# Where the delta stage takes the norms of keys and queries: from products with ones to decay exponents, value rows and the result's norm

## The chip, the cores and the metric

The kernel runs on one core of a Trainium2 chip. Its engines are TensorE (PE, matmuls, with its weight loads PEld), VectorE (DVE), ScalarE (ACT), GpSimd (POOL) and SyncE (SP, which issues DMAs). Each runs its own instructions in program order and waits on semaphores for the others. The metric is the device time of one execution in microseconds (us); several executions of a kernel are timed and the median counts.

## The reference

One layer of an encoder on 1024 tokens of width 2048. One projection feeds three groups of heads: A, a gated DeltaNet with eight heads of 128 in both directions; B, windowed attention; C, cross-attention into 256 memory tokens. The change is all in group A:

```python
def l2_norm(t):
    return t * lax.rsqrt(jnp.sum(t * t, axis=-1, keepdims=True) + EPS)
...
qa = l2_norm(qa); ka = l2_norm(ka)
...
q = q * dk ** -0.5
decay = jnp.where(incl, jnp.exp(gc_i - gc_j), 0.0)
a = -jnp.where(strict, (k * beta) @ k.T * decay, 0.0)
tinv = (I - a) ** -1
u = tinv @ (v * beta);  w = tinv @ (k * beta * jnp.exp(gc))
qk = q @ k.T * decay;   q_dec = q * jnp.exp(gc)
k_dec = k * jnp.exp(gc_last - gc)
v_new = u - w @ state;  o = q_dec @ state + qk @ v_new
state = state * jnp.exp(gc_last) + k_dec.T @ v_new
...
o_a = rms_norm(o_fwd + o_bwd, o_norm_a) * silu(za)
```

A key's norm is a factor per token. It can be left on the raw key if the decay of its column is divided by the squared norm and its value row is multiplied by the norm. A query's norm is a factor on one row of `o`, which the RMS norm of the result takes out again, up to its epsilon.

## The kernel before

`front_stage` makes the projections and stores them as tiles of 128 by 1024. `delta_stage` (from L569) takes the eight heads of group A one after another; then come the attention stage (B and C) and the output projection. Each engine's program in the delta stage is written out by hand: `heads(slot)` calls `slot(h, parity, more, before)` for the eight heads. `more` is true for h = 0 to 6 and marks that the head after this one (g = h + 1) is prepared inside the slot; `before` is true for h = 1 to 7 and marks that the head before this one is finished inside it (its RMS norm and gate). No scheduler is at work: what stands in a slot runs in that order on its engine.

A slot has two parts. The first inverts the triangular matrices of head h in six levels (L = 6). In each level TensorE multiplies four banks (`products_z`, L1240), VectorE masks them (`take_z`, L1055), TensorE multiplies again (`products_i`, L1246), and VectorE adds the result in (`take_i`, L1069) and transposes it for the next level (`turn`, L1063). The second part is a scan over eight chunks. Between these products TensorE does the work for head g, all of it in one pair of PSUM banks `pp`, and VectorE, ScalarE and GpSimd do theirs:

- ScalarE squares queries and keys (`squares`, L746); TensorE adds the squares up by a product with a tile of ones (`norm_sums`, L1178); ScalarE makes the root from Ln and Exp (`roots`, L752 and L755), and VectorE multiplies the tiles by it (`unit`, L1034). Ln and Exp come from two table sets, so an ACT_TABLE_LOAD stands before each change.
- VectorE's `columns` (L1021 to L1029) are five instructions on 8 to 32 elements per partition: they make the decay exponents of the columns. The last, `kdc`, is the exponent of the keys that go into the state.
- GpSimd's `neg_rows` (L940, two instructions) makes the decay exponents of the rows in `dec`, which ScalarE exponentiates (`decays`, L769). After it come `end` (L984, L987: the finished head times its norm, times its gate), `decayed_queries` (L950), `scaled_rows` (L959) and `first_inverse` (L968 to L974).
- The head before is finished by ScalarE squaring its result (`end_squares`, L802), TensorE's `end_sums` (L1220), ScalarE's `end_roots` (L807, L810) and `end_take` (L817), and GpSimd's `end`.

The first head has no slot before it; its preparation stands in front of `heads(slot)` on each engine. In the last slot (h = 7) ScalarE and TensorE prepare the attention stage instead of a next head (`early_squares`, `early_sums`, L837 and L1308).

## Time and profile before

| | us |
|---|---|
| median of 3 runs | 2295.89 (2295.61 to 2296.03) |
| span of the profiled execution | 2292.6 |
| delta stage, its first load issued to its last VectorE instruction | 1202.7 to 1758.9 |
| one slot, h = 1 to 6 | 60.27 |
| ScalarE busy, of the span | 667.5 |
| VectorE busy, of the span | 1058.1 |

Of the profiled execution the page gives only the span, 3.3 us less than the median; what lies around the span is not itemised. A TensorE product of 128x128 in fp32 counts as two records and takes one slot of 0.22 us at the full clock, so "x16" in a row of the trace are eight products. Times in a timeline are counted from the start of the span.

### The profile page before, as it was taken

Reading aid. Unit: us, or ns where it says so; the run is one execution under the profiler, and the core shown is the slowest. Engines: PE = TensorE matmul, PEld = TensorE weight load, DVE = VectorE, ACT = ScalarE, POOL = GpSimd, SP = SyncE. Lnnn points to the kernel's source line nnn. Section 1 sums busy time; section 2 is a strip of 40 time slices with the busy share of each in tenths; the row PEclk is TensorE's granted clock in tenths of the full one; section 3 lists DMA queues with packets and bytes.
Section 4 is the critical chain, followed back from the end, with each engine's and each line's share of the span. In section 5 each row is a group of like instructions: output and inputs, shape, how many; then the busy total and the mean of one; then the engine's idle time right before and its main releaser. Section 6 shows DMA issues by size and latency. Waiting matters only on the chain. (4 is left out here: it accounts for less than half of the span.)

```text
span 2292.6 us, 28450 instructions
## 1 busy us (share of the span) xinstructions
PE 2160.5 (94%) x11264; PEld 1800.8 (79%) x11264; DVE 1058.1 (46%) x1834; ACT 667.5 (29%) x1019; POOL 337.8 (15%) x208
## 2 busy tenths in 40 slices
PE   6999999999999999999985999999998778999998
PEld 6788888888888888888873888888886445888887
DVE  7764344354353311122315666666644887422222
ACT  6511111111111111111105455555543665311111
POOL 4300000000000000000003455555511000000000
PEclk9999999999999999999996999999979999999999
DMA  6522221221221221221203131111111333634432
GB/s 224 192 92 68 70 82 58 79 82 55 82 77 61 82 82 64 73 82 56 65 28 122 47 123 66 65 65 65 47 65 55 101 90 122 230 132 165 143 128 91
DMA packets 78866, 210.87 MB, mean 92 GB/s; under 512 B 7328, under 2 KB 33056, under 8 KB 74560
## 3 DMA queue, kind: packets, MB, share of 16 engines
q1 hardware_dynamic: 69232, 174.57, 22.9%
q0 software_dynamic: 9552, 35.19, 3.9%
q8 instruction: 53, 0.87, 0.2%
q14 instruction: 29, 0.24, 0.0%
HBM read 165.11 MB, written 44.63 MB: 91 GB/s over the span
## 5 line engine op out<-in xcount | busy, mean ns | idle before, releaser
L73 PE MATMUL pr_acc<-x_hi,pr_w_lo 128*128 128x512 f32 (+1 forms) x1760 | 675.5, 384 | 27.0 <-DVE pr_w_lo L432 24.4
L75 PE MATMUL pr_acc<-x_hi,pr_w_hi 128*128 128x512 f32 (+1 forms) x1760 | 673.9, 383 | 0.0
L74 PE MATMUL pr_acc<-x_lo,pr_w_hi 128*128 128x512 f32 (+1 forms) x1760 | 673.8, 383 | 0.0
L73 PEld LDWEIGHTS pr_acc<-x_hi,pr_w_lo 128*128 128x128 f32 x1760 | 333.6, 190 | 92.8 <-issue 18.6
L74 PEld LDWEIGHTS pr_acc<-x_lo,pr_w_hi 128*128 128x128 f32 x1760 | 333.8, 190 | 63.7 <-issue 0.2
L75 PEld LDWEIGHTS pr_acc<-x_hi,pr_w_hi 128*128 128x128 f32 x1760 | 333.7, 190 | 63.6
L348 ACT ACTIVATE pr_w_hi<-pr_w_raw 128x1024 fp32r<-128x1024 f32 x118 | 124.8, 1059 | 749.3 <-PE pr_acc L75 730.4
L533 DVE TENSOR_TENSOR pr_padded<-pr_acc,pr_rstd 128x512 f32<-128x512 f32 x82 | 56.6, 692 | 518.4 <-PE pr_acc L75 518.3
L256 POOL DMA_DIRECT2D proj_scratch<-pr_res x49 | 26.2, 535 | 1010.0 <-DVE pr_res L556 829.3
L432 DVE TENSOR_TENSOR pr_w_lo<-pr_w_raw,pr_w_hi 128x1024 fp32r<-128x1024 f32 x118 | 147.8, 1289 | 0.2 <-ACT pr_w_hi L348 0.2
L545 DVE SCALAR_TENSOR_TENSOR pr_conv<-pr_padded,pr_head_taps,pr_conv 128x1024 f32<-128x1024 f32 x96 | 123.3, 1285 | 3.4
L1240 PE MATMUL dl_ring<-dl_wt,dl_mt 128*128 128x128 f32 x768 | 107.2, 290 | 9.1 <-DVE dl_wt L1063 9.1
L1240 PEld LDWEIGHTS dl_ring<-dl_wt,dl_mt 128*128 128x128 f32 x768 | 97.0, 199 | 20.8 <-DVE dl_wt L1063 12.7
L1069 DVE TENSOR_TENSOR dl_dt<-dl_ring,dl_dt 128x256 f32<-128x256 f32 x192 | 78.9, 412 | 48.2 <-PE dl_ring L1246 45.8
L1246 PEld LDWEIGHTS dl_ring<-dl_dt,dl_wt 128*128 128x128 f32 x768 | 95.2, 198 | 7.5 <-issue 7.5
L73 PE MATMUL ou_acc<-ou_w_hi,ou_lo_rest 128*128 128x512 f32 x256 | 99.6, 389 | 0.0
L74 PE MATMUL ou_acc<-ou_w_lo,ou_hi_rest 128*128 128x512 f32 x256 | 99.6, 389 | 0.0
L75 PE MATMUL ou_acc<-ou_w_hi,ou_hi_rest 128*128 128x512 f32 x256 | 99.6, 389 | 0.0
L1246 PE MATMUL dl_ring<-dl_dt,dl_wt 128*128 128x128 f32 x768 | 98.4, 283 | 0.0
L1055 DVE TENSOR_TENSOR dl_wt<-dl_ring,c_masks 128x256 f32<-128x256 f32 x192 | 76.0, 417 | 33.7 <-PE dl_ring L1240 32.0
L533 DVE TENSOR_TENSOR pr_res<-pr_acc,pr_rstd 128x512 f32<-128x512 f32 x20 | 13.8, 692 | 167.4 <-PE pr_acc L75 167.3
L1911 DVE TENSOR_TENSOR c_ow_lo<-c_e_pair,c_ow_hi 128x2048 fp32r<-128x2048 f32 x15 | 34.4, 2294 | 121.2 <-ACT c_ow_hi L1875 121.2
(263 smaller groups left out, 2939.4 us busy)
## 6 DMA issues: line engine op xcount, KB each, us to landing
pr_w_raw<-in_w_in SPq DMA_DIRECT2D x118, 512.0 KB, 5.2
proj_scratch<-pr_res POOLq DMA_DIRECT2D x49, 512.0 KB, 5.4
c_e_more<-in_w_out SPq DMA_DIRECT2D x16, 1024.0 KB, 5.0
c_e_pair<-in_w_out SPq DMA_DIRECT2D x15, 1024.0 KB, 4.9
dl_qk<-proj_scratch SPq DMA_DIRECT2D x8, 1024.0 KB, 5.0
dl_grow<-gate_rows SPq DMA_DIRECT2D x8, 1024.0 KB, 7.6
c_e_q_in<-in_x SPq DMA_DIRECT2D x8, 1024.0 KB, 7.2
out<-c_e_kvt POOLq DMA_DIRECT2D x8, 1024.0 KB, 4.7
```

The source lines that it names most:

```text
L73: pe.matmul(out, w_lo, x_hi, start=first, stop=False)
L74: pe.matmul(out, w_hi, x_lo, start=False, stop=False)
L75: return pe.matmul(out, w_hi, x_hi, start=False, stop=last)
L348: return act.activation(w_hi[:, b], w_raw[:, b], ACT.Copy).then_inc(s_hi, 1)
L432: dve.tensor_tensor(w_lo[:, b], w_raw[:, b], w_hi[:, b].bitcast(F32), ALU.subtract).then_inc(s_lo, 1)
L533: dve.tensor_tensor(body[:, bass.ts(h, HALF)], acc[:, bank + h], rstd[:, bass.ts(h, HALF)], ALU.mult).then_inc(s_taken, 1)
L545: dve.scalar_tensor_tensor(conv[:], src, w, conv[:], ALU.mult, ALU.add).then_inc(s_tap, 1)
L1055: dve.tensor_tensor(zz[:, 2 * b:2 * b + 2], ring[:, b, 0:2 * P].rearrange("p (a n) -> p a n", n=P), masks[:, level, None, :].to_broadcast( ...
L1069: dve.tensor_tensor(left, as_blocks(ring[:, b, 0:2 * P], LEVELS[level]), left, ALU.add).then_inc(s_id, 1)
L1240: last = pe.matmul(ring[:, b, bass.ts(i, P)], mt[:, 2 * b + i], d[:, 2 * b + i], start=True, stop=True)
L1246: last = pe.matmul(as_blocks(ring[:, b, bass.ts(i, P)], LEVELS[level]), zz[:, 2 * b + i], left_d(parity, 2 * b + i, 1, level), start=True, ...
L1911: dve.tensor_tensor(w_lo[q % 2], w_raw[q % 2], w_hi[q % 2].bitcast(F32), ALU.subtract).then_inc(w_l, 1)
```

## The change

Keys and queries stay raw. Their squares are no longer summed by a product with ones.

- Keys: TensorE transposes the raw keys already at level 0 (`to_rows(g, 0)`). ScalarE reads each half twice from PSUM: once squared into the tile `kd`, which is free then, and once copied into `k_rows`. VectorE sums the squares (`key_sums`, one TENSOR_REDUCE, level 1), ScalarE takes the logarithm of the 8 sums per partition (`key_logs`), VectorE subtracts it from the column exponents and makes `kdc` (`key_columns`, two small instructions, level 2), and ScalarE makes the norm (`value_scales`), by which it multiplies the value rows, chunk by chunk (`value_rows`, now eight instructions).
- Queries: ScalarE squares them (`query_squares`), and when the head is finished GpSimd adds these squares to those of the result (`add_queries`) ahead of `end_sums`. For the last head VectorE adds them.
- One table set with both Ln and Exp is loaded before the first head; from there to the last slot no other is. ACT_TABLE_LOADs in the delta stage: 49 before, 7 now.
- `norm_sums`, `roots`, `unit` and their semaphores are gone.

The core of the diff:

```diff
             def slot(h, parity, more, before):          # ScalarE
                 g, q = h + 1, 1 - parity
-                if more:
-                    squares(g)
                 if before:
                     end_squares(h - 1)
-                if not more:
+                if more:
+                    key_rows(g, q, pp)
+                    query_squares(g, q)
+                else:
                     early_squares()
                 if more:
-                    roots(g, 1)
-                if more:
-                    roots(g, 0)
+                    key_logs(g)
                 if before:
                     end_roots(h - 1)
                     end_take(h - 1)
                 if more:
-                    key_rows(g)
+                    value_scales(g)
                     column_exps(g, q)
                     row_exps(g)
                 if more:
-                    value_rows(g, q)
+                    value_rows(g, q, pp)
                     decays(g, 0, 5)
...
+            def key_rows(g, parity, bank):
...
+                    turned = bank[:, half].rearrange("p (a n) -> p a n", n=P)
+                    act.activation(key_squares(parity)[:, 4 * half:4 * half + 4], turned, ACT.Square).then_inc(e_ksq, 1)
+                    act.activation(k_rows[:, 4 * half:4 * half + 4], turned, ACT.Copy).then_inc(e_rows, 1)
...
+            act.preload_act_table_set("natural_log_exp_and_others")
...
+            def add_queries(f, parity):                 # GpSimd
+                pool.wait_ge(f_sq, f * 2 + 2)
+                pool.wait_ge(e_sq, f + 1)
+                pool.tensor_tensor(osq[:], osq[:], root[:, parity], ALU.add).then_inc(f_ad, 1)
...
             def slot(h, parity, more, before):
+                if before:
+                    add_queries(h - 1, 1 - parity)
                 if more:
                     neg_rows(h + 1)
...
+            def key_sums(g, parity):                    # VectorE
+                dve.wait_ge(e_ksq, g * 2 + 2)
+                dve.tensor_reduce(ksum[:], key_squares(parity), AX_X, ALU.add).then_inc(e_ks, 1)
+
+            def key_columns(g):
+                dve.wait_ge(e_kln, g + 1)
+                dve.wait_ge(e_dif, g * 3 + 1)
+                dve.tensor_tensor(negc[:], negc[:], kln[:, None, :].to_broadcast([P, 2, NC]),
+                                  ALU.subtract).then_inc(e_dif, 1)
+                dve.wait_ge(e_dif, g * 3 + 2)
                 dve.tensor_tensor(kdc[:], glast[:], negc[:], ALU.add).then_inc(e_dif, 1)
...
                     if more and level == 1:
-                        unit(g, 1)
+                        key_sums(g, q)
+                    if more and level == 2:
+                        key_columns(g)
...
-                    if more and level == 1:
-                        unit(g, 0)
...
                     if more and level == 0:             # TensorE
-                        norm_sums(g, 1)
+                        to_rows(g, 0, None)
                     if more and level == 2:
-                        to_rows(g, 0, h - 1 if before else None)
+                        to_rows(g, 1, h - 1 if before else None)
...
                         if more:
-                            end_sums(h - 1, e_rt, g * 4 + 4)
+                            end_sums(h - 1, e_rows, g * 4 + 2)
...
-                    if more and level == 0:
-                        norm_sums(g, 0)
-                    if more and level == 2:
-                        to_rows(g, 1, None)
```

How the instructions stand, on VectorE in the slot of head 1 before the change, from the masking of level 0 to the adding of level 2 (`dl_wt<-dl_ring` is `take_z`, `dl_dt<-dl_ring` is `take_i`):

```order
L1055 TENSOR_TENSOR dl_wt<-dl_ring,c_masks 128x256 x4
L1021 COPY dl_hc<-c_cols 128x32
L1023 COPY dl_glast<-dl_grow 128x8
L1024 COPY dl_glast<-dl_grow 128x8
L1027 TENSOR_TENSOR dl_negc<-dl_hc 128x16
L1029 TENSOR_TENSOR dl_kdc<-dl_glast,dl_negc 128x16
L1069 TENSOR_TENSOR dl_dt<-dl_ring,dl_dt 128x64x2x2 x2
...
L1055 TENSOR_TENSOR dl_wt<-dl_ring,c_masks 128x256 x4
L1034 SCALAR_TENSOR_TENSOR dl_qk<-dl_qk,dl_root 128x1024
...
L1034 SCALAR_TENSOR_TENSOR dl_qk<-dl_qk,dl_root 128x1024
L1055 TENSOR_TENSOR dl_wt<-dl_ring,c_masks 128x256 x4
L1069 TENSOR_TENSOR dl_dt<-dl_ring,dl_dt 128x16x2x8 x2
```

The same stretch of VectorE with the change (L1078 is `take_z`, L1092 is `take_i`):

```order
L1078 TENSOR_TENSOR dl_wt<-dl_ring,c_masks 128x256 x4
L1040 COPY dl_hc<-c_cols 128x32
L1042 COPY dl_glast<-dl_grow 128x8
L1043 COPY dl_glast<-dl_grow 128x8
L1046 TENSOR_TENSOR dl_negc<-dl_hc 128x16
L1092 TENSOR_TENSOR dl_dt<-dl_ring,dl_dt 128x64x2x2 x2
...
L1078 TENSOR_TENSOR dl_wt<-dl_ring,c_masks 128x256 x4
L1050 TENSOR_REDUCE dl_ksum<-dl_kd 128x8
L1092 TENSOR_TENSOR dl_dt<-dl_ring,dl_dt 128x32x2x4 x2
...
L1078 TENSOR_TENSOR dl_wt<-dl_ring,c_masks 128x256 x4
L1055 TENSOR_TENSOR dl_negc<-dl_negc,dl_kln 128x16
L1058 TENSOR_TENSOR dl_kdc<-dl_glast,dl_negc 128x16
L1092 TENSOR_TENSOR dl_dt<-dl_ring,dl_dt 128x16x2x8 x2
```

Two passes over 1024 elements have gone and one has come; one small instruction of level 0 has moved to level 2, with a new one ahead of it.

On GpSimd, before the change, from the end of the slot of head 0 to the decayed queries in the slot of head 1 (`dl_dec` is `neg_rows`, `c_e_pair` is `end`, which works in that tile):

```order
L974 TENSOR_TENSOR dl_mt<-dl_mt 128x1024
L940 TENSOR_TENSOR dl_dec<-dl_grow,c_neg 128x1024 x2
L984 TENSOR_TENSOR c_e_pair<-c_e_pair,dl_osq 128x1024
L987 TENSOR_TENSOR c_e_pair<-c_e_pair,dl_z 128x1024
L950 TENSOR_TENSOR dl_qd<-dl_qk,dl_grow 128x1024 x2
```

And with the change:

```order
L986 TENSOR_TENSOR dl_mt<-dl_mt 128x1024
L997 TENSOR_TENSOR dl_osq<-dl_osq,dl_root 128x1024
L952 TENSOR_TENSOR dl_dec<-dl_grow,c_neg 128x1024 x2
L1002 TENSOR_TENSOR c_e_pair<-c_e_pair,dl_osq 128x1024
L1005 TENSOR_TENSOR c_e_pair<-c_e_pair,dl_z 128x1024
L962 TENSOR_TENSOR dl_qd<-dl_qk,dl_grow 128x1024 x2
```

The new addition stands ahead of the two instructions of `neg_rows`, in the slots of heads 1 to 6.

## Rows read from the trace of the kernel before

**Rows 1.** The page, its first line.

```profile
span 2292.6 us, 28450 instructions
```

**Rows 2.** Busy time in a stretch: length, then us per engine (instructions), clock, DMA.

```profile
1190.00:1700.00 510.00, 460.82 (x3421) 412.05 (x3420) 325.93 (x818) 251.55 (x424) 252.25 (x115) 0.96 0.22 75
```

**Rows 3.** Timeline of TensorE, head 1: start, duration, line [idle before <- releaser].

```profile
1306.55 1.95 PE L1240 MATMUL dl_ring<-dl_wt,dl_mt 128*128 128x128 f32 x16
1308.34 1.88 PE L1178 MATMUL dl_pp<-dl_root,c_ones 128*128 128x512 f32 x4
...
1315.94 1.99 PE L1220 MATMUL dl_pp<-dl_osq,c_ones 128*128 128x512 f32 x4 [0.30 <-ACT dl_root L752]
```

**Rows 4.** Timeline of VectorE, the same slot, levels 0 to 2.

```profile
1307.20 1.76 DVE L1055 TENSOR_TENSOR dl_wt<-dl_ring,c_masks 128x256 f32<-128x256 f32 x4
...
1310.73 0.91 DVE L1069 TENSOR_TENSOR dl_dt<-dl_ring,dl_dt 128x256 f32<-128x256 f32 x2 [1.11 <-PE dl_ring L1246]
...
1318.41 0.87 DVE L1069 TENSOR_TENSOR dl_dt<-dl_ring,dl_dt 128x256 f32<-128x256 f32 x2 [1.18 <-PE dl_ring L1246]
...
1321.19 1.18 DVE L1034 SCALAR_TENSOR_TENSOR dl_qk<-dl_qk,dl_root 128x1024 f32<-128x1024 f32 x1
...
1324.01 0.87 DVE L1069 TENSOR_TENSOR dl_dt<-dl_ring,dl_dt 128x256 f32<-128x256 f32 x2 [0.30 <-PE dl_ring L1246]
```

**Rows 5.** Timeline of GpSimd, the same slot.

```profile
1301.87 4.66 POOL L940 TENSOR_TENSOR dl_dec<-dl_grow,c_neg 128x1024 f32<-128x1024 f32 x2
1324.50 2.40 POOL L984 TENSOR_TENSOR c_e_pair<-c_e_pair,dl_osq 128x1024 f32<-128x1024 f32 x1 [17.97 <-ACT c_e_pair L817]
```

**Rows 6.** Timeline of ScalarE, the same slot.

```profile
1306.75 1.08 ACT L802 ACTIVATE dl_osq<-dl_po 128x512 f32<-128x512 f32 x2 [13.62 <-PE dl_po L1296]
...
1319.57 1.27 ACT L807 ACTIVATE dl_osq<-dl_pp,c_scalars 128x512 f32<-128x512 f32 x2
1320.85 1.28 ACT L810 ACT_TABLE_LOAD   x1
```

**Rows 7.** Timeline of GpSimd and VectorE in the slot of head 0.

```profile
1248.27 4.68 POOL L940 TENSOR_TENSOR dl_dec<-dl_grow,c_neg 128x1024 f32<-128x1024 f32 x2 [0.84 <-DMA dl_grow<-gate_rows]
1248.32 2.34 DVE L1023 COPY dl_glast<-dl_grow 128x8 f32<-128x8 f32 x1
...
1250.57 0.16 DVE L1024 COPY dl_glast<-dl_grow 128x8 f32<-128x8 f32 x1
1250.77 2.22 DVE L1027 TENSOR_TENSOR dl_negc<-dl_hc 128x16 f32<-128x16 f32 x1
```

**Rows 8.** Timeline of GpSimd and VectorE at the kernel's start.

```profile
14.67 4.36 POOL L236 TENSOR_TENSOR pr_rstd<-pr_rstd,pr_padded 128x1024 f32<-128x1024 f32 x2 [1.23 <-ACT pr_padded L360]
...
14.83 2.08 DVE L442 TENSOR_SCALAR x_hi<-pr_conv,pr_mem_nw 128x256 fp32r<-128x256 f32 x1
...
17.10 2.08 DVE L442 TENSOR_SCALAR x_hi<-pr_conv,pr_mem_nw 128x256 fp32r<-128x256 f32 x1
```

**Rows 9.** Busy time and granted clock in short stretches before and in head 0.

```profile
1216.00:1218.00 2.00, 0.19 (x1) 0.00 (x0) 0.70 (x2) 1.81 (x3) 0.50 (x1) 1.00 0.00 0
1218.00:1220.00 2.00, 0.00 (x0) 0.00 (x0) 0.68 (x1) 1.99 (x3) 0.00 (x0) 0.60 0.00 0
...
1248.00:1250.00 2.00, 2.00 (x8) 1.23 (x7) 1.77 (x2) 1.40 (x3) 1.73 (x1) 0.72 0.95 389
```

**Rows 10.** Timeline of ScalarE, VectorE and TensorE before the first slot.

```profile
1216.56 0.17 DVE L1029 TENSOR_TENSOR dl_kdc<-dl_glast,dl_negc 128x16 f32<-128x16 f32 x1
...
1220.45 4.77 ACT L769 ACTIVATE dl_dec<-dl_dec,dl_negc 128x128 f32<-128x128 f32 x16
...
1229.37 2.35 DVE L1145 TENSOR_TENSOR dl_dt<-dl_mt,c_level 128x1024 f32<-128x1024 f32 x2
...
1236.13 3.78 PE L1240 MATMUL dl_ring<-dl_wt,dl_mt 128*128 128x128 f32 x16 [7.23 <-DVE dl_wt L1063]
```

**Rows 11.** Groups of instructions: a reduction over 1024 elements, attention stage.

```profile
L1624 DVE TENSOR_REDUCE at_mx<-at_ps 128x4 f32<-128x1024 f32 x8 | 9.8, 1219 | 0.0
```

More of the change, by code:

```diff
@@ L14 @@
 from contextlib import ExitStack
+import math
 import numpy as np
@@ L906, in slot @@
                     early_rotation()
[L908 to L916 removed]
+            act.preload_act_table_set("natural_log_exp_and_others")
+            key_rows(0, 0, po)
+            key_logs(0)
+            value_scales(0)
             column_exps(0, 0)
@@ L919, in _ @@
             row_exps(0)
-            for which, dst in enumerate((k_rows, v_rows[:, 0])):
-                for half in range(2):
-                    act.wait_ge(e_tr, 2 * which + half + 1)
-                    act.activation(dst[:, 4 * half:4 * half + 4], po[:, half].rearrange("p (a n) -> p a n", n=P),
-                                   ACT.Copy, scale=0.5 if which else 1.0).then_inc(e_rows, 1)
+            value_rows(0, 0, ring)
+            query_squares(0, 0)
             heads(slot)
@@ L1128, in _ @@
             columns(0)
-            unit(0, 1)
-            unit(0, 0)
+            key_sums(0, 0)
+            key_columns(0)
             dve.wait_ge(l_on, 16)
@@ L1158, in _ @@
             dve.wait_ge(f_st, f * 16)
-            dve.wait_ge(f_sq, f * 2 + 2)
+            dve.wait_ge(e_sq, A_HEADS)
+            for half in range(2):
+                cols_ = bass.ts(half, HALF)
+                dve.wait_ge(f_sq, f * 2 + (half + 1))
+                dve.tensor_tensor(osq[:, cols_], osq[:, cols_], root[:, parity, cols_], ALU.add).then_inc(f_ad, 1)
             for half in range(2):
@@ L1372, in slot @@
                         early_rotate(1)
-            for j in (1, 0):
-                pe.wait_ge(e_sq, 1 - j + 1)
-                for half in range(2):
-                    pe.matmul((pp if j else ring)[:, half], c["ones"][:], root[:, j, bass.ts(half, HALF)],
-                              start=True, stop=True).then_inc(e_nm, 1)
-            pe.wait_ge(e_hat, E0 + 1)
+            pe.wait_ge(l_qk, 16)
+            for half in range(2):
+                for i in range(4):
+                    last = pe.transpose(po[:, half, bass.ts(i, P)], qk[:, 1, bass.ts(4 * half + i, P)], ident[:])
+                last.then_inc(e_tr, 1)
             for half in range(2):
@@ L1394, in _ @@
             pe.wait_ge(l_v, 16)
-            for which, rows in enumerate((qk[:, 1], v[:])):
-                for half in range(2):
-                    if which:
-                        pe.wait_ge(e_rows, half + 1)
-                    for i in range(4):
-                        last = pe.transpose(po[:, half, bass.ts(i, P)], rows[:, bass.ts(4 * half + i, P)], ident[:])
-                    last.then_inc(e_tr, 1)
+            for half in range(2):
+                for i in range(4):
+                    last = pe.transpose(ring[:, half, bass.ts(i, P)], v[:, bass.ts(4 * half + i, P)], ident[:])
+                last.then_inc(e_tr, 1)
+            pe.wait_ge(e_rows, 4)
             heads(slot)
```

110 lines of the change are left out of this document (48 added, 62 removed).

## Prediction, made before the changed kernel ran

> **What bounds the kernel now.** I started at the page's span [rows 1], then asked for busy time by stretch, and in the delta stage for the timelines of the engines in the slot of head 1, which heads 2 to 6 repeat every 60.27 us. TensorE is busy 460.8 of the 510 us that hold the stage's first part, VectorE 325.9, ScalarE 251.6, GpSimd 252.3 [rows 2]. That looks like a stage bound by TensorE, and over a whole slot it nearly is. But I read level by level, with S = 1306.55 as the slot's start [rows 3]. A level needs 3.6 us of TensorE (8 products in 1.79, twice) and about 4.4 us of VectorE (mask 4, add 4, transpose 4). Only where TensorE has extra work, or VectorE has, does a level take longer. So the levels are a ring through both engines, and a stall of VectorE between its masking and its adding lengthens the slot as soon as TensorE has no other work to cover it.
>
> **What goes.** `norm_sums` is two pairs of products of 1.71 us each at level 0 [rows 3]; the transposes of the keys (eight records where a group of products has sixteen, so 0.9 us) move up into one of the places. `unit` is two passes of VectorE, 1.18 to 1.22 us each, and a reduction of 1.2 us takes the place of one [rows 4, 11]. 42 ACT_TABLE_LOADs go, but ScalarE is hardly waited for inside a slot; what this is worth is seen below. If nothing else happened I get this for a slot: adding at level 0 starts at S + 3.4 instead of S + 4.2 [rows 4], level 1 at S + 9.2 instead of S + 11.9, level 2 at S + 14.5 instead of S + 17.5. A gain of 2.9 us per slot; this is a rival below.
>
> **What comes, and where it falls.** The place that decides is VectorE's `columns` at level 0, which starts when the masking ends, S + 2.35 (1307.20 + 1.76 is S + 2.41, less the overlap of neighbours) [rows 4]. Before the change GpSimd is idle then: `neg_rows` ran from 1301.87 to 1306.53, before the slot, and `end` came at 1324.50 [rows 5]. With the change `add_queries` stands ahead of `neg_rows` and waits for the squares of the result, done at S + 1.28 (1306.75 + 1.08) [rows 6]. So GpSimd works S + 1.3 to 3.7, 3.7 to 6.05 and 6.05 to 8.4 (2.34 us an instruction) [rows 7], right over `columns`.
>
> What such an overlap does is in the trace, in the slot of head 0, where `columns` falls on `neg_rows`: a copy of 8 elements takes 2.34 us and a subtraction of 16 takes 2.22 us, each until the GpSimd instruction of that moment ends; the copy behind the first one slips through in 0.16 us [rows 7]. At the kernel's start it is the same with four equal instructions under two of GpSimd: the first waits 2.08 us, the second passes, the third waits 2.08 us, the fourth passes [rows 8]. VectorE's instructions that read PSUM and one SBUF tile (masking, adding, `attention`), and its transposes, ran beside GpSimd at their usual length.
>
> The Trainium skill, page "SBUF — State Buffer", section "Who interferes with whom", says that VectorE and GpSimd share a pair of ports, that a two-port copy or an instruction with two SBUF inputs and a GpSimd instruction lock each other out for a whole instruction, and that whoever issues first wins. It speaks against this change, which puts one more GpSimd instruction first; rows 7 agree with it at 2.34 and 2.22 us. By the rule the sum is the forecast's, without it the first rival's.
>
> So with the change, at level 0: the first copy waits until S + 3.7, the second passes, the third waits until S + 6.05, and the subtraction, which waits for the copies' semaphore and starts 0.2 us behind the last one [rows 7], comes too late for the gap and waits until S + 8.4. Adding starts at S + 8.45 instead of S + 4.2.
>
> Level 1: adding and transposing take 2.66 us, masking 1.35, the reduction 1.2, so the key sums are there at T = S + 13.65. TensorE's next products start 1.15 us after adding began and are done at S + 11.6; `end_sums` (1.7 us) follows, then `products_i`, so that adding starts at S + 14.0 instead of S + 11.86 [rows 4].
>
> Level 2: `key_columns` comes 4.1 us after that (2.78 for adding and transposing, 1.33 for masking), at S + 18.1. On ScalarE `end_roots` now stands behind `key_logs`; from its first Ln to GpSimd's start it took 4.93 us with one table load of 1.28 [rows 5, 6], so 3.65 without, so GpSimd's `end` starts at T + 3.8 = S + 17.45, ahead of VectorE by 0.6 us. Both of its instructions (2.4 us each) [rows 5] stop one of the two of `key_columns`, since the second again waits for a semaphore: free at S + 22.4. Adding starts there instead of at S + 17.46 [rows 4]. Levels 3 to 5 and the scan follow as before. The loss is 4.9 us per slot, six times.
>
> Bounds of this term: if the first copy is not stopped, the subtraction gets through at S + 6.05 and the same reckoning gives +2.6 per slot; if nothing is stopped, -2.9. I take 4.9, because a copy of the same kind was stopped.
>
> **TensorE's clock.** The stalls leave TensorE without work from S + 4.6 to S + 9.6, and for some 3.6 us before level 3. In the trace an idle time that began at 1216.2 finds the mean clock at 0.60 in the stretch from 1218 on [rows 9]: it fell from 2.4 to 1.2 GHz in it. The eight products that came first after an idle time of 7.23 us took 3.78 us [rows 10] instead of 1.95 [rows 3], so at least that much work goes at 1.2 GHz; in the slot of head 0 the clock is on its way back only in the stretch from 1248 on, at 0.72 [rows 9]. For the first idle time that is 0.7 to 2.2 us, for the second 0 to 1.4, since VectorE sets the pace there. Bounds 0 to 3.6 per slot; I take 1.3, the low half, because the low clock covers a piece of one group only.
>
> **The other terms.** In front of head 0, VectorE's `columns` still ends at 1216.56 [rows 10]; then come the reduction 1.2, two small ScalarE and two small VectorE steps, together 1.2, so the 16 decays (4.77 us) start at 1218.95 instead of 1220.45 and end at 1223.7 [rows 10]. Products of keys with keys no longer wait for norms, so only the decays are waited for, and VectorE's last matrix is ready at 1224.65 instead of 1229.37 [rows 10]: -4.7 us, and the loads for head 1 come as much earlier. The table load on this path is 1.3 us of it. The value rows, now last on ScalarE, are ready at 1228.2, before the slot starts at 1231.4, and cost nothing; bounds -5 to -2. In the slot of head 0, `columns` is stopped by `neg_rows` as before [rows 7]; one `unit` goes (-1.2), two small steps come, TensorE has less to do and comes to level 1 with the clock low (+1.0): -0.2, bounds -1.5 to +2. In head 7's slot TensorE's clock falls and returns as before as far as the rows tell. Behind the last scan VectorE adds in halves ahead of each product, 0.6 us [rows 11].
>
> Sum: 6 x (4.9 + 1.3) - 4.7 - 0.2 + 0.6 = +32.9. On the span of 2292.6 [rows 1] that is 2325.5, and 3.3 us more on the median of 2295.89, which stands that far above it: 2328.8 us, 1.4% slower.
>
> **Rivals.**
> 1. No new stall: VectorE gets in between GpSimd's instructions, or these come later than I think. For it: inside the slots of heads 1 to 6 no stop was ever seen; against it, both engines' starts follow from rows, and the same two pieces of work did stop each other in head 0. Then 6 x -2.9 - 4.7 - 1.1 + 0.6 = -22.6: 2273 us. That is the change doing what it says.
> 2. Half the stops: level 0 is left at S + 6.05, no clock loss. 6 x 2.6 - 4.3 = +11: 2307 us. If `key_columns` is moreover ahead of `end` (it is 0.4 us behind in this case), one of its two stops goes, 2.4 us per slot: -3, 2293 us. This needs only half a microsecond.
> 3. The clock takes its whole price, low after both idle times in each slot: 6 x 8.5 - 4.3 = +47: 2343 us. If it stayed low through the levels, more than 2350.
> 4. ScalarE becomes late: its value rows are eight instructions of some 0.3 us instead of two, and its row exponents come behind `key_columns`. In my reckoning the value rows end at S + 27.2 and TensorE asks for them at S + 30.4; a margin of 3 us. If it fails, +1 us per slot, 2335 us, inside the range.
>
> **The numbers.** Forecast with the stops in full, clock price from 0 to 3 us: 0.56 (2318 to 2339). Rival 2, its first case: 0.17; its second, at no change or just under: 0.05. Rival 3: 0.10, of it 0.03 over 2350. Rival 4: 0.03. Rival 1: 0.09. The range from 2303 to 2348 leaves out rival 1, rival 2's second case and the top of rival 3. This kernel's measurement can tell 0.2% (4.6 us) from no change. Faster: rival 1 and a part of rival 2's second case, 0.11; within 0.2%: 0.03; slower: 0.86.
>
> **What the profile after would show.** Right: in the slots of heads 1 to 6 a VectorE copy on `glast` or `hc` of 1.4 to 2.4 us, a subtraction on `negc` of over 2 us at level 0 and one or two at level 2; slots of 65 to 68 us instead of 60.27; idle TensorE of about 5 us behind level 0 and a clock under 1.00 somewhere behind it; ScalarE with fewer busy us and nobody waiting for it. Wrong: these instructions at 0.17 us, or slots under 60 us. If they are long and the slots are still short, then my order of levels is wrong; if slots are over 69 us, the clock costs more than I took.

## The result and the profile after

The changed kernel took 2312.86 us (median of 6 runs, 2301.4 to 2314.72), the kernel before, run beside it, 2295.96 us: a ratio of 1.0067, with a 95% interval of 1.0048 to 1.0085. The change makes the kernel slower by 17 us. I had forecast +32.9 us. The direction was right, and the time lies in the range, but the loss is half of what I summed up.

The profiled execution of the changed kernel took 2312.98 us. First line of its page:

```profile
span 2311.3 us, 28308 instructions
```

That is 18.7 us over [rows 1]. The same stretch of the delta stage as in [rows 2]: length, then busy us of TensorE, its weight loads, VectorE, ScalarE and GpSimd with their instructions, granted clock, DMA share, GB/s.

```profile
1190.00:1700.00 510.00, 434.58 (x3262) 401.14 (x3261) 345.08 (x798) 164.95 (x398) 263.82 (x120) 0.92 0.20 69
```

TensorE has 26 us less work in it and ScalarE 87 us less, and still the stage is longer: VectorE is busy 19 us more with fewer instructions. Fewer instructions that take longer: that is where to look. The slots begin (first products of level 0) at 1231.44, 1302.24, 1365.95, 1430.00, 1494.45, 1557.96, 1621.69 and 1685.87, so the six middle ones take 383.6 us, 63.9 each (63.5 to 64.5), where they took 361.6, 60.27 each. The 18.7 us are:

| part | forecast | measured |
|---|---|---|
| in front of head 0 | -4.7 | -4.7 |
| slot of head 0 | -0.2 | +0.4 |
| slots of heads 1 to 6 | +37.2 | +22.0 |
| last slot and end of the stage | +0.6 | +0.3 |
| all later stages | 0 | +0.7 |

The timeline of VectorE in the slot of head 1 (start, duration, engine, line; S = 1302.24), which answers to [rows 4, 7]:

```profile
1304.57 1.44 DVE L1040 COPY dl_hc<-c_cols 128x32 f32<-128x32 f32 x1
1305.92 0.16 DVE L1042 COPY dl_glast<-dl_grow 128x8 f32<-128x8 f32 x1
1306.00 2.33 DVE L1043 COPY dl_glast<-dl_grow 128x8 f32<-128x8 f32 x1
1308.36 2.27 DVE L1046 TENSOR_TENSOR dl_negc<-dl_hc 128x16 f32<-128x16 f32 x1
1310.55 0.74 DVE L1092 TENSOR_TENSOR dl_dt<-dl_ring,dl_dt 128x256 f32<-128x256 f32 x2
...
1322.12 1.21 DVE L1055 TENSOR_TENSOR dl_negc<-dl_negc,dl_kln 128x16 f32<-128x16 f32 x1
1323.36 0.17 DVE L1058 TENSOR_TENSOR dl_kdc<-dl_glast,dl_negc 128x16 f32<-128x16 f32 x1
```

GpSimd in the same slot (the answer to [rows 5]; in brackets the idle time before an instruction and what ended it):

```profile
1303.60 2.37 POOL L997 TENSOR_TENSOR dl_osq<-dl_osq,dl_root 128x1024 f32<-128x1024 f32 x1 [6.02 <-ACT dl_osq L821]
1305.92 4.67 POOL L952 TENSOR_TENSOR dl_dec<-dl_grow,c_neg 128x1024 f32<-128x1024 f32 x2
1320.94 2.36 POOL L1002 TENSOR_TENSOR c_e_pair<-c_e_pair,dl_osq 128x1024 f32<-128x1024 f32 x1 [10.35 <-ACT c_e_pair L836]
1323.38 2.40 POOL L1005 TENSOR_TENSOR c_e_pair<-c_e_pair,dl_z 128x1024 f32<-128x1024 f32 x1
```

Read the two together by their ends. The first copy ends where `add_queries` does, the third instruction with the first of `neg_rows`, the subtraction with the second. The first of `key_columns` ends where GpSimd's first multiplication by the norm does, but the second takes only 0.17 us: it starts at 1323.36, and GpSimd's next instruction, which waits for the semaphore of the one ahead of it, at 1323.38.

TensorE, the answer to [rows 3]:

```profile
1302.24 1.95 PE L1258 MATMUL dl_ring<-dl_wt,dl_mt 128*128 128x128 f32 x16
...
1311.70 3.78 PE L1258 MATMUL dl_ring<-dl_wt,dl_mt 128*128 128x128 f32 x16 [4.71 <-DVE dl_wt L1086]
```

And its granted clock, the third number from the end of a line, in stretches of 2 us:

```profile
1310.00:1312.00 2.00, 0.30 (x1) 0.30 (x2) 2.00 (x6) 0.00 (x0) 0.59 (x1) 0.50 0.00 0
1312.00:1314.00 2.00, 2.00 (x11) 2.00 (x11) 1.78 (x6) 0.00 (x0) 0.00 (x0) 0.50 0.00 0
1314.00:1316.00 2.00, 2.00 (x8) 1.61 (x8) 1.14 (x4) 0.00 (x0) 0.00 (x0) 0.51 0.00 0
1316.00:1318.00 2.00, 2.00 (x10) 1.22 (x9) 1.07 (x2) 0.90 (x3) 0.00 (x0) 1.00 0.00 0
```

It waits 4.71 us for VectorE and comes back at 1.2 GHz (granted clock 0.50) for some 4 us; the same eight products take 3.78 us instead of 1.95. There is no second fall in the slot. The wait is 4.71 or 4.72 us in all six middle slots, but the time for which the clock stays at 0.50 after it is 3.2 to 6.2 us, and the slots follow it: the one of head 4 with 3.2 us takes 63.5 us, the one of head 3 with 6.2 us takes 64.5.

### The profile page after: what moved, and what is told of

Same layout as the page of the kernel before. It is cut to its first block and busy times, and to the rows that moved or that the text cites. A ratio compares the mean times of both kernels' runs of the same rounds, so it can differ in the third digit from the quotient of the medians.

```text
span 2311.3 us, 28308 instructions
## 1 busy us (share of the span) xinstructions
PE 2151.8 (93%) x11200; PEld 1804.9 (78%) x11200; DVE 1086.7 (47%) x1838; ACT 589.0 (25%) x1001; POOL 354.9 (15%) x215
## 5 line engine op out<-in xcount | busy, mean ns | idle before, releaser
L1258 PE MATMUL dl_ring<-dl_wt,dl_mt 128*128 128x128 f32 x768 | 122.6, 314 | 48.0 <-DVE dl_wt L1086 47.8
L1258 PEld LDWEIGHTS dl_ring<-dl_wt,dl_mt 128*128 128x128 f32 x768 | 108.4, 219 | 60.3 <-DVE dl_wt L1086 38.7
L1092 DVE TENSOR_TENSOR dl_dt<-dl_ring,dl_dt 128x256 f32<-128x256 f32 x192 | 77.8, 410 | 38.6 <-PE dl_ring L1264 36.7
L1078 DVE TENSOR_TENSOR dl_wt<-dl_ring,c_masks 128x256 f32<-128x256 f32 x192 | 74.9, 414 | 35.9 <-PE dl_ring L1258 34.8
```

The source lines that it names most:

```text
L1078: dve.tensor_tensor(zz[:, 2 * b:2 * b + 2], ring[:, b, 0:2 * P].rearrange("p (a n) -> p a n", n=P), masks[:, level, None, :].to_broadcast( ...
L1092: dve.tensor_tensor(left, as_blocks(ring[:, b, 0:2 * P], LEVELS[level]), left, ALU.add).then_inc(s_id, 1)
L1258: last = pe.matmul(ring[:, b, bass.ts(i, P)], mt[:, 2 * b + i], d[:, 2 * b + i], start=True, stop=True)
```

## The experiments

Each was run beside the kernel before, whose own runs lie in two groups, near 2282 and near 2295 us (experiment 8 goes into this). The changed kernel has such groups too: four of its six runs lie near 2313.6 us and two near 2301.6. So I read each kernel's middle slots in its trace first, and its median second. Where the clock doesn't fall in them the middle slots repeat within 0.1 us, except where I say so.

**1. Masked rows first.** Does the order on GpSimd make the loss?

```diff
-                if before:
-                    add_queries(h - 1, 1 - parity)
                 if more:
                     neg_rows(h + 1)
+                if before:
+                    add_queries(h - 1, 1 - parity)
```

> The changed kernel with two operations of GpSimd exchanged in each slot: the masked rows of the next head (neg_rows) come before the adding of the query squares (add_queries), not behind it. Theory (the 16.9 us are port stops, and what TensorE's clock loses in the idle time that they open): the masked rows run before the slot's start, as in the kernel before, and only the adding is left beside the copies of `columns`. The first copy is stopped until about S + 3.7, the other three instructions run in 0.1 to 0.2 us each, the first `take_i` adds at about S + 4.2 instead of S + 8.3, TensorE's idle of 4.72 us in level 0 goes and with it the fall of the clock to 0.50. Middle slots: 63.9 less 4.1 less 1.7 = about 58.1 us; the run about 2313 - 6 x 5.8 = 2278 us (2273 to 2288). Rival A (the loss comes from the added work itself, on VectorE's key sums and ScalarE's eight value rows, and the stops only take time that was idle anyway): the slots stay near 63.9 us, the run 2308 to 2315 us. Rival B (the stops go, but the clock falls all the same, since the slot's load on TensorE is now lighter): slots about 59.8 us, the run about 2288 us.

Measured: slots of 58.14 us, 2278.11 us (2266.95 to 2285.48, 7 runs), ratio to before 0.9929 (0.9902 to 0.9956). Of the four instructions only the first is stopped, 1.44 us; adding starts at S + 4.05 and TensorE never waits over 0.7 us in a middle slot. The theory holds to a tenth of a microsecond per slot; rivals A and B fall.

**2. A pause between the two masked-row instructions.** Why did the second of `key_columns` get through?

```diff
                 for direction in range(2):
+                    if after_first(g) and direction == 1:
+                        pool.wait_ge(e_neg, g * 2 + 1)
                     pool.tensor_tensor(dec[:, direction * NC:(direction + 1) * NC],
```

> The changed kernel with one wait added: between the two masked-row instructions of GpSimd, the second waits for the semaphore of the first (for the middle heads and head 7's slot alike). Nothing else moves. Theory (an instruction of VectorE gets through where GpSimd pauses on a semaphore, which is why only one of the two of key_columns was stopped): the pause of some 0.05 us lets the subtraction behind the copies, stopped for 2.27 us in every middle slot of the changed kernel, run in 0.1 to 0.2 us. The first `take_i` adds at about S + 6.1 instead of S + 8.3, TensorE's idle falls from 4.7 to about 2.5 us, and the slot gains 2.2 us, with the clock's 1.7 us if it no longer falls: 6 x 2.2 to 6 x 3.9 = 13 to 23 us, the run 2290 to 2300 us. Rival (the pause plays no part, the second of key_columns got through for another reason, such as its smaller size or because two stops don't follow each other): the subtraction is still stopped for about 2.3 us, the run stays at 2311 to 2314 us.

Measured: slots of 61.25 to 61.43 us, 2299.25 us (2296.01 to 2303.37). VectorE in the slot of head 1:

```profile
1306.70 2.33 DVE L1045 COPY dl_glast<-dl_grow 128x8 f32<-128x8 f32 x1
1309.06 0.18 DVE L1048 TENSOR_TENSOR dl_negc<-dl_hc 128x16 f32<-128x16 f32 x1
```

GpSimd's pair takes 4.83 us instead of 4.67, 0.16 us more, and the subtraction 0.18 instead of 2.27. One added wait on GpSimd makes the slot 2.5 us shorter, of which 2.1 us are the earlier adding (S + 6.2 instead of S + 8.3). TensorE's idle time is 2.62 us, and its clock still falls (0.50 for one stretch of 2 us in the slot of head 2), so most of the clock's price stays. The rival falls. In the slot of head 0 the same wait stands between the same two instructions, and there it doesn't help: VectorE's subtraction comes 0.06 us after GpSimd's second instruction has started, and takes 2.31 us.

**3. Keep TensorE busy in the idle time.** What does the clock cost apart from the stops?

```diff
                     for b in range(4):
                         products_i(h, parity, level, b)
+                    if more and before and level == 0:
+                        pe.wait_ge(e_rows, g * 4 + 2)
+                        for i in range(5):
+                            pe.matmul(pp[:, i % 2], c["ones"][:], qk[:, 1, 0:HALF], start=True, stop=True)
```

> The changed kernel with five products more on TensorE in each middle slot, whose results nobody reads: ones x keys, 512 columns each, behind the products of level 0 that wait for take_z, so that they fall into the idle time of 4.72 us. The stops of the port are untouched. Theory (the idle time costs twice, once as a delay and once as a clock that falls to 0.50 behind it, 1.7 us per slot as read): the granted clock stays at 1.00 between S + 8 and S + 18, the second adding comes at about S + 14.0 instead of S + 15.7, slots about 62.2 us, the run about 2313 - 10 = 2303 us (2299 to 2306). Rival (the clock's fall costs nothing, since VectorE's instructions set level 1 and not TensorE's products): the clock stays up and the run stays at 2311 to 2315 us. Second rival (the five products delay the next level's, which stand behind them in TensorE's queue): slower than 2315 us.

Measured: slots of 62.4 us, 1.5 less. The stops are untouched except in the slot of head 3, which takes 62.6 us; there GpSimd comes ahead of the second copy, so that both copies on `glast` are stopped (2.39 and 2.38 us) and the subtraction gets through in 0.18. TensorE's work in the slot of head 1, and the clock in two stretches of it:

```profile
1307.36 4.56 PE L1373 MATMUL dl_pp<-dl_qk,c_ones 128*128 128x512 f32 x10
1312.23 2.47 PE L1258 MATMUL dl_ring<-dl_wt,dl_mt 128*128 128x128 f32 x16 [0.32 <-DVE dl_wt L1086]
```

```profile
1312.00:1314.00 2.00, 1.76 (x12) 1.50 (x13) 2.00 (x7) 0.00 (x0) 0.00 (x0) 1.00 0.00 0
1314.00:1316.00 2.00, 2.00 (x11) 1.28 (x10) 2.00 (x5) 0.00 (x0) 0.00 (x0) 1.00 0.00 0
```

The eight products start at S + 9.47 (S = 1302.76 here), at S + 9.46 in the changed kernel, so the added ones delay nothing, and 1.5 us per slot is what the clock's fall costs. Both rivals fall. The median, 2294.2 us, is 19 us under the changed kernel's and not the 9 that six slots give, because the runs fall otherwise into groups: seven lie between 2291 and 2297 us and three between 2300 and 2304. Upper group against upper group the gain is about 11 us, lower against lower about 8.5. In this trace the clock of the last slot was back after 7 us, which is another matter (experiment 8).

**4. `columns` one level later.** The same question as 1, from VectorE's side.

```diff
-                    if more and level == 0:
-                        columns(g)
                     if more and level == 1:
                         key_sums(g, q)
+                        columns(g)
```

> The changed kernel with VectorE's `columns` moved one level later, behind the key sums of level 1; GpSimd's order is untouched, so add_queries and both masked-row instructions still run from S + 1.3 to S + 8.3. Theory (GpSimd's instructions cost only by the copies that they stop): level 0 then has no instruction of VectorE that shares the port, it adds at about S + 4.2, the idle of 4.72 us goes, and the copies run undisturbed behind the key sums, in about 0.6 us together, before `end` starts at about S + 17. Slots about 63.9 - 4.1 - 1.7 = 58.1 to 59 us, the run 2278 to 2284 us; `end` and key_columns keep their stop of about 1.1 us. Rival (the stops just move to level 1, because the slot is 5.8 us shorter ahead of it while GpSimd is not, so that the copies now meet the masked rows' end or `end`): a stop of 1 to 4.6 us in level 1, slots 60 to 63 us, the run 2290 to 2308 us.

Measured: slots of 57.6 us, 2261.46 us (2260.19 to 2262.57), ratio 0.9861 (0.9829 to 0.9892). VectorE in the slot of head 1:

```profile
1307.11 0.17 DVE L1040 COPY dl_hc<-c_cols 128x32 f32<-128x32 f32 x1
1307.19 0.16 DVE L1042 COPY dl_glast<-dl_grow 128x8 f32<-128x8 f32 x1
1307.27 0.16 DVE L1043 COPY dl_glast<-dl_grow 128x8 f32<-128x8 f32 x1
1307.46 0.18 DVE L1046 TENSOR_TENSOR dl_negc<-dl_hc 128x16 f32<-128x16 f32 x1
...
1311.93 1.52 DVE L1055 TENSOR_TENSOR dl_negc<-dl_negc,dl_kln 128x16 f32<-128x16 f32 x1
1313.49 0.17 DVE L1058 TENSOR_TENSOR dl_kdc<-dl_glast,dl_negc 128x16 f32<-128x16 f32 x1
```

The copies run for 0.17 us each, only a quarter of a microsecond after the end of GpSimd's last masked row (1306.85). The rival falls. The run came out 17 us under the low end of what I expected, because I had left out two things: head 0's slot also loses its stop of [rows 7] (65.48 us instead of 70.8), and the last slot's clock stayed up for most of it (80.9 us to the first products of the attention stage, 91.8 in the changed kernel).

**5. GpSimd's order alone, in the kernel before.** In the slots of heads 1 to 6; the repeated instruction's result is overwritten.

```diff
+                if before:
+                    pool.wait_ge(f_sq, (h - 1) * 2 + 2)
                 if more:
                     neg_rows(h + 1)
...
+                if 0 < g - 1 < A_HEADS - 1:
+                    pool.tensor_tensor(dec[:, NC:NT], grow[:, 0].rearrange("p (a n) -> p a n", n=P),
+                                       neg[:, 0, None, :].to_broadcast([P, NC, P]), ALU.add).then_inc(e_rep, 1)
                 for direction in range(2):
+                    if 0 < g - 1 < A_HEADS - 1 and direction == 1:
+                        pool.wait_ge(e_rep, g - 1)
```

> The kernel before, with only GpSimd's side of the change put into its slots of heads 1 to 6: neg_rows waits until the squares of the last result are done (S + 1.3), and one instruction of the same shape stands ahead of its two (it writes masked rows that are then overwritten, so it leaves out nothing and adds one instruction of 2.34 us). No norm is folded anywhere. Theory (the change's loss is this order on GpSimd and nothing else): `columns` in level 0 is stopped as in the changed kernel, a copy of about 1.4 us, one of 2.3, a subtraction of 2.3; adding starts 4.2 us later, at about S + 8.4. A slot of 60.27 becomes 64.5 if TensorE's norm products cover enough of the idle time to keep its clock, 66 if not; the run 2320 to 2331 us. Rival (the loss needs the added key sums, small steps and value rows of the change, and the order alone is covered by slack): slots under 62 us, the run below 2306 us.

Measured: slots of 64.2 to 64.4 us (one of 62.8) instead of 60.27, together +22.8 us; 2304.55 us (2302.87 to 2317.66). The loss needs nothing else of the change: it is as large as the changed kernel's 22.0. So the rival falls, though the run, at 2304.55 us, was under the limit it named and 15 us under what the theory gave: in this trace the last slot's clock was back after 3 us, which takes off about what separates the two groups. The one short slot is that of head 3. TensorE is idle as long there as in the others, 2.37 us, and the clock stays up. The clock in 3 us of it, and in the same 3 us of the slot of head 4, which takes 64.2 us:

```profile
1444.00:1447.00 3.00, 3.00 (x17) 2.15 (x17) 3.00 (x8) 2.94 (x4) 0.00 (x0) 1.00 0.00 0
1507.00:1510.00 3.00, 3.00 (x13) 2.81 (x14) 2.12 (x7) 2.41 (x3) 0.00 (x0) 0.50 0.02 5
```

So the fall costs 1.4 to 1.7 us in this kernel too, and the length of the idle time alone doesn't decide whether it comes. TensorE's idle time is 2.37 us here and 4.71 in the changed kernel, for the same stops: the norm products that the change takes out would have covered half of them. Thus the order costs 3.8 us a slot where they stand, and 6.3 us (63.9 less 57.6) where they are gone.

**6. Two table sets again.**

```diff
-            act.preload_act_table_set("natural_log_exp_and_others")
```

> The changed kernel without its one table set for ScalarE in the delta stage: logarithms and exponentials load their tables by turns again, at 1.28 us a load, two loads a slot (ahead of key_logs, and between the logarithms and the exponential of end_roots). All else is the changed kernel. Theory (ScalarE isn't waited for inside a slot, so the table set is worth only what stands on the path in front of head 0): +1.3 to +2.6 us in front of head 0; in the slots `end` on GpSimd starts up to 2.6 us later and so behind key_columns, whose stop of 1.1 us goes: 0 to -0.6 us a slot. The run 2310 to 2316 us. Rival (the loads stand on the path from the key sums to key_columns and the decay exponents): +1.3 to +2.6 us a slot, the run 2320 to 2330 us.

Measured: 2321.85 us (2308.65 to 2324.6), 9 us over the changed kernel; both theory and rival missed in part. The first slot starts 3.6 us later, but 2.6 of that lie ahead of the part that was changed: GpSimd's first masked rows of head 0 start at 1214.69 instead of 1212.05. From there to the first slot it is 20.4 us instead of 19.4, so one load of 1.28 us on the path costs 1.0. The slots: 62.94 us for head 1, with `key_columns` ahead of GpSimd, as the theory had it; 65.0 for the others, where GpSimd got there first. VectorE, and under it GpSimd, in head 2:

```profile
1389.10 2.16 DVE L1054 TENSOR_TENSOR dl_negc<-dl_negc,dl_kln 128x16 f32<-128x16 f32 x1
1391.29 0.17 DVE L1057 TENSOR_TENSOR dl_kdc<-dl_glast,dl_negc 128x16 f32<-128x16 f32 x1
...
1388.87 2.35 POOL L1001 TENSOR_TENSOR c_e_pair<-c_e_pair,dl_osq 128x1024 f32<-128x1024 f32 x1 [11.73 <-ACT c_e_pair L836]
```

The loads move GpSimd's start closer to VectorE's, in this slot from 1.5 us ahead to 0.2 ahead, and the stop gets longer, not shorter. So they cost by where they put another engine's start. In the traces this one table set is worth 5.3 us to the changed kernel (4.3 in the middle slots, 1.0 in front), in the medians up to 9; both are more than I gave it.

**7. `end` in half widths.** The step that failed in the forecast, brought about on purpose.

```diff
-                pool.tensor_tensor(fin[:], fin[:], osq[:], ALU.mult).then_inc(f_n, 1)
-                pool.wait_ge(f_n, f + 1)
-                pool.wait_ge(l_z, f * 16 + 16)
-                pool.tensor_tensor(fin[:], fin[:], z[:, parity], ALU.mult).then_inc(f_res, 1)
+                halves = [slice(0, HALF), slice(HALF, SEQ)]
+                pool.wait_ge(l_z, f * 16 + 16)
+                pool.tensor_tensor(fin[:, halves[0]], fin[:, halves[0]], osq[:, halves[0]], ALU.mult).then_inc(e_half, 1)
+                pool.tensor_tensor(fin[:, halves[1]], fin[:, halves[1]], osq[:, halves[1]], ALU.mult).then_inc(f_n, 1)
+                pool.wait_ge(e_half, f * 2 + 1)
+                pool.tensor_tensor(fin[:, halves[0]], fin[:, halves[0]], z[:, parity, halves[0]], ALU.mult).then_inc(e_half, 1)
+                pool.wait_ge(f_n, f + 1)
+                pool.tensor_tensor(fin[:, halves[1]], fin[:, halves[1]], z[:, parity, halves[1]], ALU.mult).then_inc(f_res, 1)
```

> The changed kernel with GpSimd's two multiplications of `end` cut into four of half the width, in the order first half, second half by the norm, then first half, second half by z, so that only the last of the four waits for a semaphore of the instruction right ahead of it. The step that failed in the forecast was that both instructions of key_columns would be stopped. Theory (the second got through because GpSimd paused on its own semaphore just then): the first, which arrives about 1.2 us into the pair, now ends with the second quarter, where GpSimd goes on without a pause, so the second instruction of key_columns is stopped for about 1.2 us instead of 0.17. Slots about 1.0 us longer, 64.9 us, the run 2313 + 6 = 2319 us. Rival (it got through because it is another size or because an instruction behind a stopped one always passes): 0.17 us again, the run 2310 to 2315 us.

Measured: slots of 64.85 to 64.95 us, 2320.07 us (2316.92 to 2320.6). VectorE and GpSimd in the slot of head 1:

```profile
1322.79 1.03 DVE L1059 TENSOR_TENSOR dl_negc<-dl_negc,dl_kln 128x16 f32<-128x16 f32 x1
1323.86 1.19 DVE L1062 TENSOR_TENSOR dl_kdc<-dl_glast,dl_negc 128x16 f32<-128x16 f32 x1
...
1322.52 1.27 POOL L1005 TENSOR_TENSOR c_e_pair<-c_e_pair,dl_osq 128x512 f32<-128x512 f32 x1
1323.75 1.27 POOL L1007 TENSOR_TENSOR c_e_pair<-c_e_pair,dl_z 128x512 f32<-128x512 f32 x1
```

The theory's 1.2 us and 64.9 us came, and the run lies 1 us over its 2319. Where GpSimd goes on without a pause (1323.75, ahead of 1323.86) the same instruction is stopped that went through in 0.17 us before. With experiment 2 this settles the step from both sides.

**8. No stop at all, and the last slot.** Three kernels: the candidate; the kernel before with three products in the last slot; the candidate with them.

```diff
# the candidate: experiment 4, and
                 for level in range(L):
+                    if more and level == 2:
+                        key_columns(g)
                     for b in range(4):
                         take_z(h, level, b)
-                    if more and level == 2:
-                        key_columns(g)
# and in early_norms
-                act.preload_act_table(ACT.Ln)
# the three products, in TensorE's program
+                    if not more and level == 3:
+                        pe.wait_ge(a_kln, 2)
+                        for i in range(3):
+                            pe.matmul(pp[:, 1], c["ones"][:], masks[:, 0:4].rearrange("p a n -> p (a n)"),
+                                      start=True, stop=True)
```

> The candidate: the changed kernel with `columns` behind the key sums of level 1 (as in the run with columns in level 1), key_columns ahead of the masking of level 2, where GpSimd's `end` hasn't begun yet, and without the separate load of a logarithm table in the last head's slot (the set of the stage has it). Theory: no instruction of VectorE is stopped in a middle slot; the idle of 0.52 us in level 2 goes, slots 57.1 us instead of 57.6; in the last slot one load of 1.28 us less stands ahead of the exponential that TensorE's early sums wait for, idle there about 1.0 us instead of 2.31. Run about 2261 - 3 - 1.3 = 2257 us (2253 to 2260 where the clock of the last slot stays up, some 10 us more where it falls for 25 us). Rival (key_columns moved ahead meets a logarithm that isn't ready, since key_logs follow the key sums by only 1.5 us on ScalarE, or delays the masking by as much as it saves): slots 57.6 to 59 us, the run 2260 to 2270 us.

Measured: slots of 57.03 us, no instruction of VectorE stopped in them (`key_columns` in 0.13 and 0.17 us). TensorE's idle time in the last slot is 1.03 us instead of 2.31. The run took 2262.76 us (2249.09 to 2263.53, 4 runs), a ratio of 0.985 (0.9805 to 0.9895): three runs at 2262 to 2264 us and one at 2249.09. So the slots came as in the theory, but the median doesn't, because the clock of the last slot stays down: 0.50 for 24 us in the trace, a run of 2263.46 us. The mean granted clock of the three slower runs is 0.975 or 0.976, that of the fourth 0.983.

> The kernel before with three products more in the last head's slot, whose results nobody reads: ones x masks, 512 columns each, behind the products of level 3 there, where TensorE is idle for 2.41 us. Nothing else is changed. The runs of the kernel before lie in two groups, at about 2282 and at about 2295 us, and in the profiled run of the slower kind the granted clock is 0.50 for 25 us of that slot, from this idle time on. Theory (the idle time lets the clock fall, and how long it stays down makes the two groups): the clock no longer falls there, all runs lie at about 2281 to 2285 us. Rival A (the clock falls because of the early sums behind it, products of 1 or 2 columns, not because of the idle time): two groups again, a median near 2295 us, or 2296 with the products' own 0.3 us. Rival B (the two groups come from another part of the kernel): the same two groups, while the last slot's clock stays up.

Measured: 2283.82 us (2280.62 to 2285.2, 5 runs), the kernel before beside it 2294.65 us (2292.67 to 2297.92), ratio 0.9948 (0.9935 to 0.9962). The last slot, first of the kernel before, then with the three products:

```profile
1688.00:1696.00 8.00, 5.59 (x37) 5.40 (x36) 2.08 (x5) 5.53 (x6) 2.36 (x1) 0.80 0.71 239
1696.00:1720.00 24.00, 24.00 (x115) 24.00 (x115) 6.56 (x17) 5.80 (x9) 0.00 (x0) 0.50 0.14 49
```

```profile
1688.00:1696.00 8.00, 8.00 (x56) 6.28 (x54) 3.35 (x10) 5.49 (x6) 2.36 (x1) 1.00 0.70 232
1696.00:1720.00 24.00, 23.48 (x203) 22.64 (x203) 8.45 (x22) 8.10 (x13) 0.00 (x0) 1.00 0.14 46
```

Both are busy throughout, but one does 115 products in 24 us and the other 203. Three products that nobody reads, put into an idle time of 2.41 us, are worth 11 us. All five runs lie where the lower group of the kernel before does; rivals A and B fall. No trace of a run of that lower group was taken, but the mean granted clock of each run is on record: 0.979 to 0.985 in the nine runs of the kernel before between 2278 and 2285 us, 0.974 to 0.978 in all but one of its others (2291.4 us, 0.981). Some 27 us at 0.50 in the last slot, as in the trace, take 0.006 off the mean by my estimate.

> The candidate without stops (columns and key_columns moved, one logarithm table fewer), with the same three products more in the last head's slot, where this kernel's TensorE is idle for 1.03 us; their results aren't read. Three of four runs of the candidate stood at 2263 us and one at 2249; in the profiled one, of the first kind, the clock was 0.50 from 1664 to 1688 us. Theory (the idle time decides whether the clock stays down): the products cost 2.6 - 1.0 = 1.6 us at most and keep the clock, all runs at about 2250 us. Rival (the early sums of 1 or 2 columns let it fall, as the short idle of 1.03 us, which is less than half of that of the other kernels, hints): 2262 to 2265 us as before, or two groups.

Measured: 2252.11 us (2251.0 to 2256.65, 5 runs), ratio to the kernel before 0.982 (0.9806 to 0.9833). This beats both kernels: 42.5 us under the kernel before, run beside it, and 61 under the changed one's median above. The rival falls: the early sums are still there and the clock stays up. In the candidate without the products the clock fell behind only 1.03 us of idle time, while in experiments 3 and 4 it fell behind 2.87 and 2.31 us and was back after 6.8 and 3.4 us. Why it stays down for 24 us or more in some runs and not in others I can't say; the idle time alone doesn't tell, and the products of one or two columns behind it were not tried apart.

## Why the forecast was half right

**What goes, and the base without a stop.** I had 60.27 - 2.9 = 57.4 us for a slot. The candidate has 57.03. This part held.

**Stops in level 0.** All four instructions behaved as forecast, in each of the six slots, and adding started at S + 8.3 (forecast S + 8.45). By my working that is worth 4.0 us of a slot, and the clock 1.3. Measured together: 63.9 - 57.6 = 6.3 us, of which 1.5 are the clock (experiment 3). The two terms were 1.0 us too low together. The Trainium skill, page "SBUF — State Buffer", section "Who interferes with whom", has GpSimd and an instruction of VectorE that is a two-port copy or reads two SBUF inputs lock each other out for a whole instruction, the first to issue winning; the 2.33 and 2.27 us here and the two experiments with GpSimd's pause (0.18 against 2.27 us, 1.19 against 0.17) agree with it.

**`key_columns`: the step that failed.** The forecast said that "Both of its instructions (2.4 us each) [rows 5] stop one of the two of `key_columns`, since the second again waits for a semaphore". From S + 18.1 to S + 22.4 it counted about 3.9 us, after the 0.4 that the two take unhindered. Two things were wrong. The smaller is that VectorE comes 0.9 to 1.5 us behind GpSimd, not 0.6, and so is stopped for the rest of the first instruction only, 1.5 to 0.9 us. The larger is that the second gets through. I had asked whether VectorE's instruction waits for a semaphore, as the subtraction in level 0 does, and not whether GpSimd's does. In `end` it does, and GpSimd's pause is enough. What the step costs is 57.6 - 57.03 = 0.6 us a slot, read between experiments 4 and 8 (a stop of 1.52 us and none), and 1.0 us more as soon as the pause is moved away (experiment 7). The reckoning per slot: base -0.4, level 0 and clock +1.0, `key_columns` -3.3, together -2.7; forecast 66.5, measured 63.9. Six times 2.6 us is the 15 us by which the middle slots miss the forecast.

**Clock.** I allowed for two falls and took 1.3 us. The first came, at 1.5 us on average; the second needed the idle time ahead of level 3 that the failed step would have made, and didn't come.

**In front of head 0.** -4.7 us as forecast, in this pair of traces. The steps came where the forecast put them: the decays start at 1219.07 (forecast 1218.95), and VectorE's last matrices are there at 1224.62 (forecast 1224.65). What is partly luck is the figure of the kernel before. Counted from GpSimd's first masked rows, the first slot starts after 19.4 us in all eight kernels that have the changed kernel's code there, but after 22.8, 23.0 and 24.3 us in the three that have the code before, and [rows 10] is from the last of these. So the change gains 3.4 to 4.9 us here. A slip without effect: 1216.56 in [rows 10] is where `columns`' last instruction starts, and it ends 0.17 us later.

**Rivals.** Rival 1 (no stop) is refuted for this kernel and is what experiments 4 and 8 made of it: the change does bring its 3 us per slot once no copy meets GpSimd. Of rival 2 the first case had the wrong place: it let the subtraction of level 0 through, which was stopped in every middle slot, though its 2307 us was nearer than my forecast. Its second case had the right place and another reason: it took one stop off `key_columns` by letting VectorE come ahead of `end`. VectorE came behind, and GpSimd's pause let the second instruction through. With VectorE ahead, as in the slot of head 1 in experiment 6, neither is stopped. Rival 3 and rival 4 didn't occur: ScalarE's value rows are eight instructions with 2.15 us together, and in the middle slots nobody waits for them.

## What to carry to other kernels

When two engines stop each other, the price depends on the microsecond at which each issues: write down for both engines where an instruction follows the one ahead at once and where it waits for its semaphore, since the other engine gets in at such a pause. Before moving work to GpSimd, look for VectorE's short instructions inside the time it will run, and move these (here that made a slot 6.9 us shorter, 63.9 to 57.0). And products taken off TensorE may have been the cover of a stall or what held its clock.

## What the runs showed of the chip

- A wait that GpSimd adds on its own last instruction lengthened its pair by 0.16 us and shortened VectorE's stopped instruction from 2.27 to 0.18 us. Where VectorE came 0.06 us after the pause, in the slot of head 0, it was stopped for 2.31 us all the same.
- The stopped instruction was released at the end of a GpSimd instruction each time, however small it is itself: 1.19 us with half-width instructions of 1.27 us on GpSimd, 2.27 us with full ones. The copy right behind a stopped one mostly got through, in 0.16 us, but not always: in one slot of experiment 3 it was stopped too, for 2.39 us.
- TensorE's clock stood at 0.50 for 24 us with the engine busy throughout (1696 to 1720 in the kernel before), behind an idle time of 2.41 us; elsewhere it was back 3 to 6 us after one of 4.71. Behind the same 2.37 us it fell in five slots of experiment 5 and not in the sixth. With this one stretch at full clock all five runs of experiment 8's second kernel came out at 2281 to 2285 us, where the lower of the two groups of the kernel before lies.
